# A diffusion backbone on one core: the first norm rearranged over TensorE, VectorE and GpSimd, and a spare weight buffer at the group ends

## What is computed

```python
def _rmsnorm(x, w):
    xf = x.astype(jnp.float32)
    y = xf * lax.rsqrt(jnp.mean(xf * xf, axis=-1, keepdims=True) + NORM_EPS)
    return (y * w.astype(jnp.float32)).astype(x.dtype)
def _modulate(h, shift, scale):
    return h * (1 + scale) + shift
...
    sc = jax.nn.silu(c)
    sc_ctx = jax.nn.silu(c_ctx)
    for i in range(DEPTH):
        sh1, sc1, g1, sh2, sc2, g2 = jnp.split((sc @ ada_w[i] + ada_b[i])[:, None, :], 6, axis=-1)
        h = _modulate(_rmsnorm(x, norm1_w[i]), sh1, sc1)
        ...   # layer 0: retention, 4 heads; layer 1: neighbourhood attention, 16 heads
        x = x + g1 * y
        h2 = _modulate(_rmsnorm(x, norm2_w[i]), sh2, sc2)
        x = x + g2 * _conv_ffn(h2, ffn_w_up[i], ffn_conv_w[i], ffn_conv_b[i], ffn_w_down[i])
    return _rmsnorm(x, final_norm_w)
```

## Time and profile before

| what | value |
|---|---|
| median of three executions | 2045.12 us (2044.84 to 2045.16) |
| the profiled execution, whole | 2049.3 us |
| its span, first to last instruction | 2047.4 us |
| TensorE matmul busy | 2005.9 us, 98% of the span |
| VectorE busy | 1329.1 us, 65% |
| ScalarE busy | 735.8 us, 36% |
| GpSimd busy | 96.5 us, 5% |
| granted TensorE clock, mean | 0.993 |

### The profile page before, as it was taken

How to read it: one execution, slowest core, us unless ns; L and a number is a source line. 1 busy time by engine, 2 the same in 40 slices (tenths; PEclk the granted TensorE clock), 3 DMA queues, 4 the chain that set the end, 5 groups by cost and what they waited for, 6 DMA issues and landing times.

```text
span 2047.4 us, 30513 instructions
## 1 busy us (share of the span) xinstructions
PE 2005.9 (98%) x10834; PEld 1720.8 (84%) x10834; DVE 1329.1 (65%) x2238; ACT 735.8 (36%) x1267; POOL 96.5 (5%) x162
## 2 busy tenths in 40 slices
PE   8999999999999999999999999999999999999998
PEld 7888888888888888888888888788888778788886
DVE  7875635735645677765664567877877777567375
ACT  5423223223313343312331233555655444233233
POOL 0000000000000000000000000211111000000000
PEclk8999999999999999999999999999999999999999
DMA  7221311321221113233224224311111222222222
GB/s 295 78 98 62 114 62 53 103 72 62 80 96 55 60 58 106 92 124 113 92 93 133 103 97 150 121 47 42 56 46 36 93 82 93 92 99 96 93 93 102
DMA packets 51260, 186.45 MB, mean 91 GB/s; under 512 B 5680, under 2 KB 5680, under 8 KB 51184
## 3 DMA queue, kind: packets, MB, share of 16 engines
q1 hardware_dynamic: 37744, 136.73, 19.3%
q0 software_dynamic: 13440, 48.63, 7.0%
HBM read 181.15 MB, written 4.19 MB: 91 GB/s over the span
## 4 chain that ended last, share of the span: by engine, by line
PE 86%; DVE 7%; issue 3%; ACT 2%; DMA 1%; SPq 0%; DVEq 0%; ACTq 0%; POOLq 0%
PE acc L401 59%; PE o_ps L523 3%; PE o_ps L559 3%; PE acc L707 3%; PE acc L649 3%; PE o_ps L692 2%; PE acc L523 2%; PE acc L546 2%; PE o_ps L707 2%; PE acc L488 2%; PE acc L742 1%; DVE pt_lo L1717 1%; PE acc L682 1%; PE o_ps L674 1%; PE o_ps L453 1%
## 5 line engine op out<-in xcount | busy, mean ns | idle before, releaser
L857 ACT ACTIVATE w_hi<-raw 128x1024 fp32r<-128x1024 f32 x229 | 242.0, 1057 | 609.0 <-PE acc L401 496.0
L1246 DVE TENSOR_TENSOR w_lo<-raw,w_hi 128x1024 fp32r<-128x1024 f32 x229 | 280.1, 1223 | 269.4 <-ACT w_hi L857 267.3
L401 PE MATMUL acc<-h_hi,w_hi 128*128 128x512 f32 x1520 | 436.0, 350 | 3.0 <-ACT u L1045 1.8
L401 PE MATMUL acc<-h_hi,w_lo 128*128 128x512 f32 x1520 | 435.4, 349 | 0.0
L401 PE MATMUL acc<-h_lo,w_hi 128*128 128x512 f32 x1520 | 434.0, 349 | 0.0
L401 PEld LDWEIGHTS acc<-h_hi,w_hi 128*128 128x128 f32 x1520 | 244.9, 188 | 43.5 <-ACT u L1045 2.6
L401 PEld LDWEIGHTS acc<-h_lo,w_hi 128*128 128x128 f32 x1520 | 244.2, 188 | 39.5
L401 PEld LDWEIGHTS acc<-h_hi,w_lo 128*128 128x128 f32 x1520 | 243.8, 188 | 38.5
L1408 DVE SCALAR_TENSOR_TENSOR x<-acc,mod,x 128x512 f32<-128x512 f32 (+3 forms) x136 | 81.9, 636 | 145.0 <-PE acc L401 134.0
L401 PE MATMUL acc<-act_hi,w_hi 128*128 128x512 f32 (+1 forms) x396 | 120.1, 357 | 0.0
L401 PE MATMUL acc<-act_hi,w_lo 128*128 128x512 f32 (+1 forms) x396 | 119.4, 355 | 0.0
(11 more groups left out here) (254 smaller groups left out, 3557.3 us busy)
## 6 DMA issues: line engine op xcount, KB each, us to landing
raw<-in_weights_dram SPq DMA_DIRECT2D x232, 512.0 KB, 3.2
ada_raw<-in_ada_dram POOLq DMA_DIRECT2D x80, 512.0 KB, 3.5
ada_start<-in_ada_first_dram SPq DMA_DIRECT2D x8, 1024.0 KB, 19.3
x<-in_x_in_dram SPq DMA_DIRECT2D x4, 768.0 KB, 7.5
park_dram<-x POOLq DMA_DIRECT2D x1, 2048.0 KB, 8.1
rel<-in_bias_dram POOLq DMA_DIRECT2D x16, 128.0 KB, 2.4
x<-park_dram POOLq DMA_DIRECT2D x2, 1024.0 KB, 6.6
out_dram<-x SPq DMA_DIRECT2D x8, 256.0 KB, 2.1
```

The costliest lines, as they stand in the source:

```text
L401: mm = nc.tensor.matmul(tile[:, c0:c0 + cn], wt[:, b * P:(b + 1) * P], mv[:, n, c0:c0 + cn], start=(n == 0 and m == 0), stop=(n == last an ...
L857: nc.scalar.activation(w_hi[i][:, :] if spare is None else spare[0], raw[r][:, :], ACT.Copy).then_inc(hi_split, 1)
L1246: nc.vector.tensor_tensor(lo, raw[r][:, :], hi.bitcast(F32), ALU.subtract).then_inc(lo_split, 1)
```

## The change

What it does, part by part:

1. **Conditioning rows.** The two broadcast loads and the `Silu` over 128x2048 go. `silu_c` (128x16, made by ScalarE from the constants) is spread by TensorE: 16 matmuls of the column, broadcast, with the identity give the rows in `acc0` and `acc1`; VectorE copies both to `silu_rows`.
2. **Squares.** They go through four scratch buffers and not two; VectorE adds up six, the last two are summed by TensorE directly (`first_sums`).
3. **Rows shared out.** `PE_SHIFTS` is (0, 1, 2, 7) instead of (1, 2, 4, 6, 7). The shifts of blocks 3, 4 and 5 and the scale of block 7 are made by GpSimd (two products of 128x1024 each) and ScalarE (the sums, with `accum_out`); VectorE keeps seven scales and one shift.
4. **Roots by GpSimd.** The product of `x` and `ss` for the eight blocks moves from VectorE to GpSimd.
5. **Other norms.** The table of the root is loaded while the last tile is still awaited (`load_root`); the last block is added and squared in two halves (`x_half`, `sq_half`), and VectorE starts on the first 512 tokens when four of six spread blocks are there (`spread_half`). `keep_busy` now uses 512 columns of weights that are already split; three of its calls are shorter by one. `idle` is the old form. The last pair of attention heads gets six filler matmuls ahead of a wait.
6. **Group ends.** The last block of a group is taken out of the loop, and the chunk of the group's second output tile goes to a spare buffer there; `outputs_start` takes all blocks but the last for both tiles, and then the last block for each.

The diff, cut to its core:

```diff
-PE_SHIFTS = (1, 2, 4, 6, 7)
+PE_SHIFTS = (0, 1, 2, 7)
+POOL_ROWS = ((3, 1), (4, 1), (5, 1), (7, 0))
...
-            for c in range(2):
-                sp.dma_start(silu_rows[:, c, :], cond_rows[c, :].partition_broadcast(P)).then_inc(rows_in, 16)
...
-            pool.wait_ge(start_rows, 1)
+            def rooted_x(k):
+                if k >= 2:
+                    pool.wait_ge(h_made, k - 1)
+                nc.gpsimd.tensor_tensor(S[2 + k % 2][:, 0:TOK], x[:, k, :], ss[:, :], ALU.mult).then_inc(norm_t, 1)
+            def row(r):
+                k, which = POOL_ROWS[r]
+                place = ada_start[k][:, which, :]
+                pool.wait_ge(ada_start_in[k], 16)
+                if r >= 2:
+                    pool.wait_ge(rows_summed, 2 * r - 3)
+                nc.gpsimd.tensor_tensor(row_mul[r % 2][:, :], place, silu_rows[:, 1, :], ALU.mult).then_inc(rows_mul, 1)
+                nc.gpsimd.tensor_tensor(place, place, silu_rows[:, 0, :], ALU.mult).then_inc(rows_mul, 1)
+            pool.wait_ge(rows_done, 2)
+            pool.wait_ge(spread_copied, 1)
+            for k in range(3):
+                rooted_x(k)
+            for r in range(3):
+                row(r)
+                rooted_x(r + 3)
+            row(3)
+            rooted_x(6)
+            rooted_x(7)
+            pool.wait_ge(h_lo_done, KC)
...
+                for c in range(2):
+                    for k in range(KC):
+                        mm = nc.tensor.matmul(acc[c][:, k * P:(k + 1) * P], silu_c[:, k, c:c + 1].to_broadcast([P, P]), ident,
+                                              start=True, stop=True)
+                mm.then_inc(rows_made, 1)
...
+                for k in PE_SHIFTS[:3]:
+                    shift_row(k)
+                    idle(3, None, acc[0][:, 0:P])
...
-                        if first and k == 4:
-                            keep_busy(9, None, o_ps[:, 0, P:2 * P])
-                            shift_row(PE_SHIFTS[4])
+                        if first and k == 3:
+                            shift_row(PE_SHIFTS[3])
...
-                some(1, 0, 2)
+                some(1, 0, size - 1)
                 some(0, size - 1, size)
-                some(1, 2, size)
+                some(1, size - 1, size)
...
+            def last_square(i, after, width):
+                half = LAT if width == TOK else LAT // 2
+                act.wait_ge(sq_added, squares_added.up() - 2)
+                act.wait_ge(x_half, x_halves.up())
+                nc.scalar.activation(S[1][:, 0:half], x[:, KC - 1, 0:half], ACT.Square).then_inc(sq_half, 1)
+                act.wait_ge(acc_taken[i], after)
+                nc.scalar.activation(S[1][:, half:width], x[:, KC - 1, half:width], ACT.Square).then_inc(sq_done, 1)
...
+                def sum_row(r):
+                    k, which = POOL_ROWS[r]
+                    for n, z in enumerate((row_mul[r % 2][:, :], ada_start[k][:, which, :])):
+                        act.wait_ge(rows_mul, 2 * r + 1 + n)
+                        nc.scalar.activation(z, z, ACT.Copy, accum_out=row_sums[:, r, 1 - n:2 - n]).then_inc(rows_summed, 1)
...
-                def rooted_x(k):
-                    nc.vector.tensor_tensor(S[2 + k % 2][:, 0:TOK], x[:, k, :], ss[:, :], ALU.mult).then_inc(norm_t, 1)
...
+                for k in range(KC):
+                    if (k, 0) not in POOL_ROWS:
+                        dve.wait_ge(ada_start_in[k], 16)
+                        row(k, 0, k, one_over if k == 0 else None)
+                    if k == 0:
+                        split()
+                    else:
+                        low(k - 1)
                     shift(k)
...
-                    with turns(dve, size - (n == 0), A.steps(2) + steps) as f:
+                    with turns(dve, size - 1 - (n == 0), A.steps(2) + steps) as f:
                         inner(f + 1 if n == 0 else f, 2)
+                    inner(size - 1, 1, spare3 if layer else spare1)
```

More of the change, by code:

```diff
@@ L366, in _ @@
             A = AccLine()
-            chunk, diags = Tally(), Tally()
+            chunk, diags, halves = Tally(), Tally(), Tally()
             squares_added, h_split, p_split, gates_split, act_split = (Tally() for _ in range(5))
@@ L447, in token_sums, with spread_roots @@
                 mm.then_inc(sums_done, 1)
-            def spread_roots(parts):
+            def spread_roots(parts, twice=False):
                 pe.wait_ge(roots_ready, diags.up())
@@ L454, in spread_roots, with idle @@
                                           start=True, stop=True)
+                    if twice and t == LAT // P - 1:
+                        mm.then_inc(spread_half, 1)
                 mm.then_inc(spread_done, 1)
-            def keep_busy(n, what=None, place=None):
+            def idle(n, what=None, place=None):
                 what = ident if what is None else what
@@ L461, in keep_busy, with final_sums @@
                     nc.tensor.matmul(o_ps[:, 2, 0:P] if place is None else place, what, what, start=True, stop=True)
-            def final_sums(width):
+            def keep_busy(n, w=None, place=None):
+                w = w_hi[slot[0]] if w is None else w
+                for _ in range(n):
+                    nc.tensor.matmul(o_ps[:, 2, :] if place is None else place, w[:, 0:P], w[:, 0:LAT], start=True, stop=True)
+            def final_sums(width, ends=False):
+                if not ends:
+                    pe.wait_ge(lo_split, chunk.now() + 1)
+                half = LAT if width == TOK else LAT // 2
                 pe.wait_ge(sq_added, squares_added.up(KC) - 1)
@@ L470, in final_sums @@
                 keep_busy(4)
-                pe.wait_ge(sq_done, squares_added.now())
+                pe.wait_ge(sq_half, halves.up())
                 for t in range(width // P):
+                    if t == half // P:
+                        pe.wait_ge(sq_done, squares_added.now())
                     mm = nc.tensor.matmul(sums[:, 2 * t:2 * t + 2], S[1][:, t * P:(t + 1) * P], ones[:, 0:2],
@@ L1046, in inner @@
                         ins.then_inc(acc_taken[i], 1)
+                        if spare is not None and j == 0:
+                            split(spare)
                     act.wait_ge(conv_done, convs.now() + (layer + 2))
@@ L1284, in start_norm, with row @@
                 own_shift = lambda k: mod[:, 0, k, :]
-                def row(k, r, made):
+                def row(k, r, made, between=None):
                     place = ada_start[k][:, r, :]
@@ L1401, in norm, with add_gated @@
                 h_split.up(2)
-            def add_gated(m, layer, gate, parts):
+            def add_gated(m, layer, gate, parts, twice=False):
                 i, tile = wait_full()
+                if twice and len(parts) == 1:
+                    parts = ((0, LAT // 2, 0), (LAT // 2, LAT // 2, 0))
                 for c0, cn, c in parts:
@@ L1417, in out_projection @@
                 for m in range(KC):
-                    add_gated(m, 0, 16, PARTS)
+                    add_gated(m, 0, 16, PARTS, final and m == KC - 1)
                     if m % 2:
@@ L1654, in ffn @@
                         for m in range(2):
-                            add_gated(6 + m, layer, 40, parts)
+                            add_gated(6 + m, layer, 40, parts, m == 1)
                             if not ends:
```

220 lines of the change are left out of this document (143 added, 77 removed).

## The result

The changed kernel takes 2055.82 us (median of 5, 2055.39 to 2056.74), the kernel before 2045.16 beside it: **0.5% slower**, ratio 1.0049, 95% interval 1.0038 to 1.0060. The forecast was 2041.9, range 2016 to 2048. The profiled execution of the change took 2055.9 (span 2053.9), the usual time for it; that of before, 2049.3, lay 4.2 over its median, and the kernel before scatters: in four sessions its executions go from 2041.7 to 2049.6. So the two profiles show 6.5 us of the 10.7.

A forecast was written before the change was run, and what follows sets the result against it. TensorE was taken as busy 98% of the span, with the start set by VectorE. Start +5.3, other norms -4.7, group ends -3.7 sum to -3.1: 2045.1 to 2042.0, taken as 2041.9 us, range 2016 to 2048.

The forecast's parts named there:

- the lock: At the start, VectorE with two SBUF inputs and GpSimd reading SBUF block each other for whole instructions; costs about +5 us.
- (b): Rival for the start: no lock to speak of, values end at 63.0, time 2018.4 us; chance 0.25.
- (c): Rival for the start: lock only for products and differences, not the multiply-and-sum; time 2025.8 us; chance 0.17.
- The start up to the copy: Start of the kernel, until `ss` is copied: 3.7 us earlier, the copy ending at 20.8.
- The shared phase: After the copy, VectorE's 28.5 and GpSimd's 31.2 us take turns, 4 given back by handovers: 55.7 us.
- The tail: End of the start, where nothing is shared: GpSimd's last products wait for `h_made`, then ACT to `h_lo`: 5 us.
- the +5.3: Whole start: values end at 86.6 instead of 81.34 us.
- The other norms: Norms after the start: -3.0 before the first FFN, -0.5 before attention, -0.8 second FFN, -0.4 last; sum -4.7 us.
- Group ends: Ends of FFN groups: waits for `act_lo`, restarts and clock give -5.8, new waits for `x` +2.1; sum -3.7 us.
- Gains of clock that the forecast counted: TensorE's granted clock no longer falling: 1.7 us behind the last group end; a faster spread, 1.17, before the first FFN.
- The rival on the other side: Rival (d), start: GpSimd holds the port longer, no handover gain; values end at 92.4, 2050.9 us; chance 0.10.

The follow-up runs named there:

- experiment 7: Changed kernel with all GpSimd's used products back on VectorE or otherwise off GpSimd, plus 16 unused 128x1024 products on GpSimd: 2086.37 us (one execution).
- experiment 8: Changed kernel with no used products on GpSimd, plus 16 memsets of 128x1024 there, which only write: 2055.93 us (one execution).
- Experiment 10: Changed kernel, but VectorE adds up all eight squares and TensorE makes 12 column sums, not 36: 2052.97 us, ratio 1.0038 to the kernel before.
- experiment 1: The kernel before again, unchanged, with a second profile: 2048.75 us, span 2046.8.
- Experiment 9: Changed kernel with the group ends of the kernel before in both FFNs: 2058.80 us, ratio 1.0065 to the kernel before.
- experiments 2 to 12: Eleven variants of the changed kernel, some with parts undone and some with instructions added, each timed beside the kernel before: 2040.48 to 2086.37 us.

## Why the prediction was wrong

**What bounds the kernel, and the lock: right.** TensorE waits for `h_lo`; the two engines exclude each other, in both directions, also for the multiply-and-sum, which was the open point. Rivals (b) and (c) are out: in experiment 7, 16 unused products cost their whole length, and the multiply-and-sum takes up to 3.40. The price of the lock was right too. What VectorE's held-up instructions took beyond their lengths alone sums to 27.6 us in the changed kernel (multiply-and-sums 8.7, `h_lo` 8.0, TENSOR_SCALARs 10.9); the forecast was 31.2 - 4 = 27.2.

One reading behind it was wrong. The 0.15 at 1332.12 was not "alone": GpSimd's product had started at 1332.10, so that place shows only that VectorE isn't always held up. And the rows held one thing that was not read, that a TENSOR_SCALAR is held up as well: `prob<-prob,top` took 0.80 beside GpSimd and 0.58 here:

```profile
1332.10 2.14 POOL L339 TENSOR_TENSOR bias<-rel,masks 128x192 f32<-128x192 f32 x3 [8.93 <-DVE top L1697]
...
1332.50 0.58 DVE L1707 TENSOR_SCALAR prob<-prob,top 128x640 f32<-128x640 f32 x1
```

The Trainium skill (SBUF — State Buffer, "Who interferes with whom") says that a GpSimd instruction that only writes does not contend with VectorE's second input; experiment 8 agrees for products (0.95) and multiply-and-sums (1.22). The same section of the Trainium skill says that `tensor_scalar` may enter a mode that uses the shared pair of ports; the 1.15 of a 128x2 beside a memset agrees.

**The start up to the copy: this step failed.** I put the copy's end at 20.8; it was 25.30 (24.49 + 0.81). The term of 3.7 us gained counted a table load, a multiply-and-sum and an earlier load as gone from the path, and gave the 24 added column sums no price ("summed by TensorE directly" stood in the change, and in no term of the sum). They took 5.26 us, at half clock, after three pauses of 1.43, 0.35 and 0.35 us between 9.5 and 13.1 with fillers of 0.71 between them, and the fillers and the spread behind them had 0.50 and 0.60 of the clock. Experiment 10 takes the sums out, has full clock there, and gets 3.7 of the error of 4.5 back.

**The shared phase: 55.7 forecast, 59.1 measured.** VectorE was at work from the copy at 25.3 to 82.5, 57.2 us, with six of the eight `h_lo`; the two that came later, which the forecast counted here, add 1.9. The sum had only VectorE's instructions with two inputs. It left out the small ones, two TENSOR_SCALARs a block (0.13 and 0.19 from start to start, 2.2 for seven blocks), and the 0.9 from the copy to 26.18, in which VectorE waits for TensorE's first shift: 3.1 of the 3.4.

**The tail: 5 forecast, 5.2 measured** (7.1 from 82.5 to 89.6, less the two `h_lo`). But it was right by chance: the sums that ScalarE makes of GpSimd's row I had priced at 0, "beside", and the last pair, 2 x 1.04, stands between two blocks (VectorE waits 0.99 for it), while the first of the two times 2.2 ran beside VectorE's split. With 0.8 of clock that was not lost at the end: 4.5 + 3.4 + 0.2 - 0.8 = 7.3 more than the +5.3. These shares are worked out from one profile; experiment 10 tests only the first.

**The other norms: -4.7 forecast, -1.9 in the profile.** Before the first FFN -1.4 in the profile, against -3.0. The eleven variants with the new norms have 53.1 or 53.2 there, so the gain is 1.9 or 2.9, by which profile of before (55.1, 56.0) it is measured; in both the spread ran at half clock (2.77). But its first term, the table load of 1.28, was never on the path. It ran from 717.27 to 718.55 beside TensorE's sums, which ended at 719.35 (in the profile of experiment 1 both end at 717.0); that row of PE was not read. What is gained is the half clock's share and `spread_half`; no run parts the two. The last norm gave 0.2, the one before the last FFN 0.3 to 0.4 where 0.8 was forecast.

**Group ends: -3.7 forecast, right in the profile.** Without its norm the last FFN is 3.9 shorter there. The waits for `act_lo` are gone, the new ones for `x` are 0.20 to 0.25 (forecast 0.3 to 0.4). Experiment 9 gives 3.0 in the medians and 2.4 in this FFN: its clock stayed at 1.00 behind the pause, so the 1.7 of clock in the forecast was not there to be gained.

**The sum against the median.** 12.6 - 6.1 = 6.5 in the profiles, 10.7 in the medians. The rest, 4.2, is before's own: its profiled executions had a granted clock of 0.993 and 0.992, of its 42 others in experiments 2 to 12, 37 had 0.994 to 0.997. The five others at 0.992 or 0.993 took 2047.8 to 2049.6 us; but at 0.994 alone they go from 2041.7 to 2048.2, so the clock is not all of it. Gains of clock that the forecast counted (1.7 at the last group end, 1.2 in the norm) exist only in the executions that lose it. That this is the whole 4.2 is argued, not shown: no fast execution of before left a trace.

**The rival on the other side** was right in sign and place (d: values end at 92.4; measured 93.9; 2050.9 forecast, 2055.8 measured), wrong in its reason: GpSimd was no slower than 1.7 and 2.2, and the handovers gave back some 3.6. The row of 39.23 ends at 42.03, 1.7 behind the VectorE instruction that held it up (37.06 to 40.35), and a held-up `norm_a` takes 2.2, one whole product of 1024 columns. The rival was given 0.10, because every path to a late end was sought behind the copy and none ahead of it.

## What to carry to other kernels

Work moved from VectorE to GpSimd is not taken off if both read SBUF: the engines take turns, a product costs GpSimd's longer time, and a tiny instruction in line waits for a whole one of the other engine. Price every instruction that an edit adds to an idle engine as well, at the clock that engine will have by then, and the small instructions of the engine that sets the pace. Read a variant's gain by stage before its total: here a loop that moved by a few instructions hid 4 to 9 us.
